# Per-layer embedding: tanh, gating product and residual sum kept in the gate's PSUM bank

## The reference

```python
ple = jax.nn.sigmoid(x @ ple_w_gate[i] + ple_b_gate[i]) * (p[i] @ ple_w_proj[i])
x = layer_norm(ALPHA * x + ple, ln_g[i, 3], ln_b[i, 3])
```

## Time and profile before

| | us |
|---|---|
| median of 3 runs | 1572.77 (1572.47 to 1575.34) |
| the profiled execution | 1573.2 |
| its span, first to last instruction | 1571.1 |
| PE busy in the span | 1531.6 (97%) |
| DVE busy | 958.8 (61%) |
| ACT busy | 808.0 (51%) |
| POOL busy | 310.3 (20%) |

### The profile page before, as it was taken

One profiled execution on the slowest core, in us unless ns is written; L12 is line 12 of the kernel. 1 busy time (PEld: TensorE's weight loads), 2 busy tenths in 40 slices (PEclk: granted clock), 3 DMA queues, 4 the chain that ended last, 5 costly groups with the idle time before them and its releaser, 6 DMA issues.

```text
span 1571.1 us, 27635 instructions
## 1 busy us (share of the span) xinstructions
PE 1531.6 (97%) x11752; PEld 1409.1 (90%) x11752; DVE 958.8 (61%) x1351; ACT 808.0 (51%) x1247; POOL 310.3 (20%) x160
## 2 busy tenths in 40 slices
PE   7999999999999989999999999999989999999998
PEld 7999898989998879998898889998779889898896
DVE  4555467576655475554567585555477677766646
ACT  5444365455544355544573554544465565555572
POOL 0000153103000240000442040000430235503352
PEclk9999999999999999999999999999999999999999
DMA  9555463225555455555542145555455234553341
GB/s 349 212 191 190 162 221 123 82 108 216 189 186 188 166 192 212 188 188 188 201 157 100 55 170 206 188 188 188 161 201 188 108 108 161 201 189 135 108 162 54
DMA packets 41113, 266.28 MB, mean 169 GB/s; under 512 B 4444, under 2 KB 6492, under 8 KB 10784
## 3 DMA queue, kind: packets, MB, share of 16 engines
q1 hardware_dynamic: 40272, 261.18, 46.3%
q0 software_dynamic: 720, 3.35, 0.5%
HBM read 263.46 MB, written 1.05 MB: 168 GB/s over the span
## 4 chain that ended last, share of the span: by engine, by line
PE 86%; DVE 9%; ACT 3%; issue 1%; DMA 1%; SPq 0%; DVEq 0%
PE PS L483 15%; PE PS L484 15%; PE PS L485 15%; PE PS L497 6%; PE PS L499 5%; PE PS L498 5%; PE PS L535 4%; PE PS L538 4%; PE PS L536 4%; DVE rawL L315 2%; PE PS L1236 2%; PE PS L581 1%; PE PS L466 1%; PE PS L467 1%; PE PS L468 1%
## 5 line engine op out<-in xcount | busy, mean ns | idle before, releaser
L483 PE MATMUL PS<-xTH,WH 128*128 128x256 f32 x2272 | 648.3, 285 | 0.0
L484 PE MATMUL PS<-xTL,WH 128*128 128x256 f32 x2272 | 636.7, 280 | 0.0
L485 PE MATMUL PS<-xTH,rawL 128*128 128x256 f32 x2272 | 633.4, 279 | 0.0
L312 ACT ACTIVATE WH<-raw 128x1024 fp32r<-128x1024 f32 (+2 forms) x476 | 484.0, 1047 | 131.5 <-PE PS L538 101.3
L315 DVE TENSOR_TENSOR rawL<-raw,WH 128x1024 fp32r<-128x1024 f32 (+1 forms) x379 | 467.9, 1263 | 96.6 <-ACT WH L312 96.3
L315 POOL TENSOR_TENSOR rawL<-raw,WH 128x1024 fp32r<-128x1024 f32 (+1 forms) x97 | 248.7, 2582 | 1034.3 <-ACT WH L312 1034.3
L483 PEld LDWEIGHTS PS<-xTH,WH 128*128 128x128 f32 x2272 | 427.3, 188 | 9.2 <-issue 6.7
L484 PEld LDWEIGHTS PS<-xTL,WH 128*128 128x128 f32 x2272 | 426.9, 188 | 3.4 <-issue 2.9
L485 PEld LDWEIGHTS PS<-xTH,rawL 128*128 128x128 f32 x2272 | 429.5, 189 | 0.0
L312 ACT ACTIVATE sg<-PS 128x256 f32<-128x256 f32 x80 | 30.7, 383 | 193.7 <-PE PS L485 193.7
L315 DVE TENSOR_TENSOR hh<-PS,sg 128x256 f32<-128x256 f32 x80 | 33.9, 424 | 157.8 <-ACT sg L312 157.5
(11 more groups left out here) (349 smaller groups left out, 2024.3 us busy)
## 6 DMA issues: line engine op xcount, KB each, us to landing
raw<-in_weights SPq DMA_DIRECT2D x233, 1024.0 KB, 4.8
gb<-in_lngb SPq DMA_DIRECT2D x16, 512.0 KB, 4.9
raw<-in_weights SPq DMA_DIRECT2D x2, 1056.0 KB, 4.8
gb<-in_ln SPq DMA_DIRECT2D x4, 512.0 KB, 4.4
cst<-in_consts POOLq DMA_DIRECT2D x1, 1378.5 KB, 8.5
x0T<-in_xT SPq DMA_DIRECT2D x4, 256.0 KB, 6.8
raw<-in_weights SPq DMA_DIRECT2D x4, 256.0 KB, 6.3
xt<-in_x POOLq DMA_DIRECT2D x1, 1024.0 KB, 15.4
```

The source lines that it names most:

```text
L312: return Q.put("act", waits, lambda e: e.activation(out, in_, func, **kw))
L483: e.matmul(out, c, xTH[:, k, :], start=k == 0, stop=False)
L484: e.matmul(out, c, xTL[:, k, :], start=False, stop=False)
L485: ins = e.matmul(out, u.L(i, 128 * k, 128), xTH[:, k, :], start=False, stop=k == KD - 1)
```

## The change

The tile `pz` goes. Tanh reads the gate's bank and writes the same bank; the product with `pj` reads and writes that bank; the residual sum reads it and writes it, as before. The waits, the order on every engine and the number of instructions stay as they were.

```diff
     def ple(l, nxt, start):
-        z = at(f"pz{l}", [128, 2, 2, 512], F32, over)
         pj, pj_ready = ple_pj[l]
...
         def total(t, n, tok, between=lambda: None):
-            zz, b = z[:, t, n, :], 4 + 2 * t + n
+            b = 4 + 2 * t + n
+            zz = PS[:, b, :]
             yn = xt[:, t, 512 * n:512 * n + 512]
             table(TBL_EXP_TANH)
-            a = act(zz, PS[:, b, :], ACT.Tanh, [tok], scale=0.5)
+            a = act(zz, zz, ACT.Tanh, [tok], scale=0.5)
             a = stt(zz, zz, 1.0, pj[:, t, 512 * n:512 * n + 512], ALU.add, ALU.mult, [a, pj_ready[t, n]])
             between()
-            return stt(PS[:, b, :], yn, 2.0 * ALPHA, zz, ALU.mult, ALU.add, [a])
+            return stt(zz, yn, 2.0 * ALPHA, zz, ALU.mult, ALU.add, [a])
```

## The result

| | before | after |
|---|---|---|
| median of 5 runs, us | 1572.77 (1571.83 to 1575.39) | 1561.81 (1558.70 to 1564.65) |
| ratio | | 0.9935, 95% interval 0.9915 to 0.9956 |
| the profiled execution, us | 1573.2 | 1561.81 |
| its span, us | 1571.1 | 1559.7 |

The change saves 10.96 us, with an interval from 6.9 to 13.4 us (1572.77 times the distance of each end from 1). The forecast of 1563.8 is 2 us high and inside the range.

A forecast was written before the change was run, and what follows sets the result against it. PE was taken as the bound (86% of the chain), losing time in two waits on `xt` of 4.98 and 5.05 us. Savings of 6.14 + 2.85 = 9.0 us gave 1563.8 us, range 1562.3 to 1567.7.

The forecast's parts named there:

- The reading of the earlier trace: At embedding ends, DVE instructions with both tensors in SBUF wait for POOL; product took 1.73 us, sum 2.75.
- Product and sum: The t=1, n=1 pair ending each embedding: 0.696 us per instruction, 3.07 us saved a layer, 6.14 together.
- Price of the bank: Tanh writing PSUM and DVE reading it, in the embeddings: taken as zero.
- The upper end: Tanh reading and writing one bank in turns: up to 0.57 us a layer, 1.1 in all.
- PE's clock: Half-speed work behind PE's two `xt` waits, 1.385 + 1.465 us lost, taken as won: 2.85 us.
- the premise that a wait of 2 us is over before the clock falls: PE's two `xt` waits shrink to 1.91 and 1.98 us, ending before the clock falls; 2.85 us won.
- rival 1: Clock falls all the same in or just behind the shorter `xt` waits; only 6.14 us gained, 1566.6; chance 0.16.
- Over 4 us: At layer 0's `xt` wait, the granted clock falls over 4 us after the wait began at 580.12.
- rival 2: Gain eaten later, layer 1's part and the clock's lost; layer 0's 3.07 us left, 1569.7; chance 0.06.
- rival 3: Product and sum still wait for POOL, PSUM prices added: 1574.0, or 1576.9 with two more clock falls; chance 0.04.
- Both stated marks: New PE waits on `rawL`, `xTL` or loads for rival 2; a maximum staying over 1.5 us for rival 3.
- the low end of the range: Forecast less the clock fall near 840, which other timing may spare, at 1.47 us: 1562.3.

The follow-up runs named there:

- one-operand kernels: Kernel before with half of the change: only the sum, or only the product, reads its second input from the bank; 1565.77 and 1563.38 us.
- kernels with POOL idle: Kernel before and kernel after, each without POOL's four low parts at the ends of the embeddings; 1560.92 and 1559.75 us.
- second repeat of before: Kernel before, unchanged, the second of two new single executions; 1568.8 us.
- last of after: Kernel after, unchanged, a third look in a single execution; 1561.42 us.
- the repeat: Kernel after, unchanged, run once more beside new runs of the kernel before; 1563.69 us, ratio 0.9948.
- four idle sums: Kernel after with four extra DVE additions ahead of the last norm of each embedding; 1571.27 us, ratio 0.9994.
- two idle sums: Kernel after with two extra DVE additions ahead of the last norm of each embedding; 1567.69 us, ratio 0.9965.
- kernel with the product in the bank: Kernel before with tanh into the bank, product from bank and `pj` into `pz`, sum from two SBUF tensors; 1563.38 us, ratio 0.9929.

## Why the prediction was right

**What was slow and why.** The reading of the earlier trace rows held: an instruction of DVE with two SBUF tensors waits out the instruction that POOL is running. The one-operand kernels show the wait's end (0.55 and 0.56 us behind POOL's chunk), the kernels with POOL idle show that nothing else was in it. One figure of the reading was off: POOL's two chunks were taken as equal, 2.66 us each. They take 2.55 and 2.81, so the first ends at 578.70, and the slow product ends 0.56 us behind it (not 0.45), just as the slow sum does behind the second:

```profile
576.15 2.55 POOL L315 TENSOR_TENSOR rawL<-raw,WH 128x1024 fp32r<-128x1024 f32 x1 [2.24 <-ACT WH L312]
```

```profile
578.66 2.81 POOL L315 TENSOR_TENSOR rawL<-raw,WH 128x1024 fp32r<-128x1024 f32 x1
```

The Trainium skill, "SBUF — State Buffer", section "Who interferes with whom", states the rule: a DVE instruction with two SBUF inputs contends with a GpSimd instruction that reads SBUF, and one with at most one SBUF input, outside its 2-port perf modes, doesn't; the runs agree, with 1.58 and 1.01 us for the one kind beside 0.69 for the other.

**Product and sum: 6.14 us forecast, 6.12 measured** (3.05 + 3.07). Each took 0.70 where 0.696 was taken; the waits were forecast at 1.91 and 1.98 and came out at 1.92 and 1.98.

**Price of the bank: zero taken, zero found.** The product's median rose from 686 to 694 ns, the sum's fell from 699 to 696 and the tanh's from 593 to 587; ACT's line in the view of the banks:

```profile
L312 ACT ACTIVATE PS<-PS x8: 578/587/592, 564.9 to 1143.2; 128x512 f32<-128x512 f32 x8
```

The upper end, reading and writing one bank in turns, fell away. By the rule of the Trainium skill, "Perfetto Trace Analysis", section "Optimizing Scalar/DVE Operations", the estimate was 88 ns a layer; the rows have 8 more and 3 and 6 less, and the stage with POOL idle is 28.68 us in either form.

**PE's clock: 2.85 us forecast.** In the profiled pair no fall follows the shorter waits, and the term comes out at 2.49 us: 1.24 behind layer 1's wait (208.10 against 206.86), 1.25 behind layer 0's, where 1.465 and 1.385 were taken. Half the time at the low clock is thus a little more than what is lost. The second repeat of before and the last of after have the same rate in the feed-forward behind layer 0 and differ by 1.56 (186.34 and 184.78), but in that repeat the clock fell behind the restart, and its whole low stretch lay in busy work.

The step that holds only in part is the premise that a wait of 2 us is over before the clock falls. In 3 of 10 such waits the clock fell just behind the restart, in busy work, and took 1.5 us (186.33 and 208.39 in the repeat, against 184.77 and 206.86). "Over 4 us" after the wait's start was the figure of one execution; with four idle sums it was 2.4. And the argument against rival 1, that the fall near 840 belongs to small matmuls, missed PE's wait of 1.60 us ahead of it; which of the two brought that fall, no run separates. Rival 1 is thus no other outcome of the change but a part of its executions.

The price before isn't fixed either. By the same stages, less 3.1 us where the slower rate ran, it was 2.5, 4.8 (190.03 and 209.50) and 2.9 us (186.34 and 208.16) in the three executions, 3.4 in the mean. After the change 3 of 10 waits with a fall at 1.55 us leave 0.9 for the two layers. So the two terms are worth 6.12 + 3.4 - 0.9 = 8.6 us in the mean, not 9.0 (an estimate from these rows). The stage behind layer 1 is a rough measure of a fall: with two idle sums and a fall it took 207.33 us, 0.47 above the kernel after, and in the kernel after with POOL idle, without a fall, 206.09.

**The rest of 10.96.** The change accounts for 6.12 + 1.24 and 1.25 = 8.6 us of the profiled pair's 11.39; the other 2.8 are the feed-forward's rate, 3.1, less 0.3 net in other stages. The prediction had no such term: it took every stage without an edit as constant, while the executions of one kernel lie 6 us apart (1558.70 to 1564.65 after). In the repeat the difference was 9.3 us (1572.99 against 1563.69). The forecast lies inside both intervals, but that the total agrees to 2 us is partly luck and says less than the stages of the embeddings, which agree to 0.02 us each.

**Rivals 2 and 3.** Layer 1 gained 3.07 as layer 0 did, so nothing was eaten later (rival 2). No product or sum was above 0.70 us (rival 3). Both stated marks were absent.

**A miss without a price.** POOL's two chunks were forecast as long as before or 0.1 us shorter; they are 0.58 shorter (4.74 against 5.32). The wait had gone both ways. In the kernel after the two take 2.40 and 2.38 us. In the kernel before they take 2.55 and 2.81, and each starts while DVE is still at an instruction with two SBUF inputs (the sum of n=0 to 576.45, the product to 579.25). In the kernel with the product in the bank, too, the second chunk takes 2.83 us (from 580.56), as the slow sum does its work at its start. POOL is on no path here, so the total doesn't show it. The fall of the clock near 840, which the low end of the range assumed could be spared, did not simply go: it was absent in the mixing of layer 1 and there in that of layer 0, for -1.55 and +1.30 us.

## What to carry to other kernels

Where a short DVE instruction shows a maximum far above its median, look at what POOL runs at that time, and at how many of the instruction's tensors come from SBUF: putting one of them in a bank that is held anyway frees it at next to no cost in DVE or ACT time (8 ns on the product here). Count a wait of TensorE twice, once for its length and once for the clock behind it, and take the second as a chance with a price that varies (1.2 to 2.6 us here), not as a sum. Measure a gain of a few microseconds in the stage it belongs to, as the total of one kernel moves by as much from one execution to the next.

## What the runs showed of the hardware that was not expected

- The same stream of feed-forward matmuls runs at one of two rates, 5.44 or 5.68 us a unit, at a granted clock of 1.00 in both, and changes within a stage only where four transposes interrupt the stream; a stage is 1.6 us (first seven units) or 3.1 us (the other thirteen) longer for it. What chooses the rate is open.
- The granted clock fell to half just behind waits of 1.9 to 3.4 us in 5 of 16 cases, while PE was busy again, and behind none of two of 1.5 us; after 4.8 us and more in all 8. In the mixing phases it fell behind 15 of 26 waits of 1.5 to 1.8 us, so a short wait is no safe one.
- DVE's wait for POOL is POOL's wait too: two chunks take 4.74 us beside instructions with one SBUF tensor, and 5.32 beside those with two.
